# Attention's output projection as three single passes with high and low parts

## The reference

```python
h = h + 0.5 * swiglu(rms_norm(h, g_ffn1), w1_gate, w1_up, w1_down)
h = h + hybrid_mixer(rms_norm(h, g_mix), ...)      # ends in: return o @ w_out
h = h + 0.5 * swiglu(rms_norm(h, g_ffn2), w2_gate, w2_up, w2_down)
...
# second block, much later, needs
ada = silu(c) @ ada_w + ada_b                      # 1024 x 6144 weights
```

## Time and profile before

| what | us |
|---|---|
| median of three runs | 1572.23 |
| lowest, highest | 1571.33, 1572.71 |
| the profiled execution | 1573.47 |
| span of its trace | 1571.5 |
| PE busy in it | 1459.9 (93%) |
| DVE busy | 1049.8 (67%) |
| ACT busy | 546.4 (35%) |
| POOL busy | 563.6 (36%) |

### The profile page before, as it was taken

The page is one execution under the profiler, slowest core; times in us unless marked ns, Lnnn a source line. Parts: engine busy times, 40 slices in busy tenths (PEclk is TensorE's granted clock), DMA queues, the critical chain, the costliest instruction groups (busy, mean ns, idle before and its releaser), DMA issues.

```text
span 1571.5 us, 22748 instructions
## 1 busy us (share of the span) xinstructions
PE 1459.9 (93%) x8272; PEld 1120.8 (71%) x8272; DVE 1049.8 (67%) x2170; ACT 546.4 (35%) x1128; POOL 563.6 (36%) x382
## 2 busy tenths in 40 slices
PE   8999999999999999999999999998988988888777
PEld 7999998767999999998989985444444443333333
DVE  6655376875734328998976468785858585858556
ACT  5444353363544436443134242221212121212114
POOL 2455428220344441001002234554545444444451
PEclk9999999999999999999999999999999998999999
DMA  9888958996999997999976969999999999999996
GB/s 365 312 329 317 348 217 338 315 326 241 407 372 371 376 376 294 374 398 342 362 281 226 401 244 403 404 427 427 427 427 426 427 427 427 427 427 427 426 428 267
DMA packets 99814, 571.91 MB, mean 364 GB/s; under 512 B 11536, under 2 KB 11664, under 8 KB 50448
## 3 DMA queue, kind: packets, MB, share of 16 engines
q1 hardware_dynamic: 61056, 298.15, 51.3%
q0 software_dynamic: 37520, 268.47, 40.7%
q10 hardware_dynamic: 1152, 4.16, 0.7%
HBM read 569.67 MB, written 135.27 MB: 449 GB/s over the span
## 4 chain that ended last, share of the span: by engine, by line
PE 57%; DMA 26%; DVE 6%; SPq 5%; POOL 3%; issue 2%; ACT 1%; ACTq 0%; POOLq 0%; DVEq 0%
DMA arena<-pairs,eidx 15%; PE ps L2727 10%; PE ps L2113 8%; PE ps L2112 8%; PE ps L2111 8%; DMA ring<-pairs,eidx 6%; PE ps L2504 5%; SPq L664 3%; PE ps L2200 2%; PE ps L2198 2%; PE ps L2199 2%; DMA arena<-in_ada 2%; POOL w_lo L754 2%; SPq L663 2%; PE ps L2619 2%
## 5 line engine op out<-in xcount | busy, mean ns | idle before, releaser
L2727 PE MATMUL ps<-arena 128*128 128x512 f32 x844 | 402.6, 626 | 69.1 <-ACT arena L1252 69.1
L2727 PEld LDWEIGHTS ps<-arena 128*128 128x128 f32 x844 | 165.8, 201 | 289.0 <-issue 192.8
L1965 DVE CUSTOM_DVE_ANT_0 arena<-arena 128x1024 f32<-128x1024 f32 x211 | 255.2, 1225 | 145.3 <-DMA arena<-pairs,eidx 144.1
L822 POOL DMA_INDIRECT arena<-pairs,eidx x210 | 244.3, 1163 | 257.1 <-PE ps L2727 208.4
L754 POOL TENSOR_TENSOR w_lo<-ring,w_hi 128x1024 fp32r<-128x1024 f32 x76 | 207.9, 2738 | 257.7 <-DVE w_lo L1305 171.3
L2111 PE MATMUL ps<-u_hi,w_hi 128*128 128x256 f32 (+1 forms) x912 | 259.4, 284 | 1.8 <-POOL w_lo L754 1.5
L2113 PE MATMUL ps<-u_hi,w_lo 128*128 128x256 f32 (+1 forms) x912 | 259.6, 285 | 0.0
L2112 PE MATMUL ps<-u_lo,w_hi 128*128 128x256 f32 (+1 forms) x912 | 259.2, 284 | 0.0
L842 ACT ACTIVATE w_hi<-ring 128x1024 fp32r<-128x1024 f32 x188 | 197.8, 1056 | 149.7 <-PE ps L2200 71.2
L2111 PEld LDWEIGHTS ps<-u_hi,w_hi 128*128 128x128 f32 x912 | 172.1, 189 | 3.2 <-issue 2.3
L2113 PEld LDWEIGHTS ps<-u_hi,w_lo 128*128 128x128 f32 x912 | 172.3, 189 | 0.0
(11 more groups left out here) (394 smaller groups left out, 2505.3 us busy)
## 6 DMA issues: line engine op xcount, KB each, us to landing
ring<-in_stream SPq DMA_DIRECT2D x121, 1024.0 KB, 7.0
pairs<-in_peer_u SPq DMA_DIRECT2D x128, 512.0 KB, 7.5
pairs<-in_peer_v SPq DMA_DIRECT2D x128, 512.0 KB, 8.6
arena<-in_ada SPq DMA_DIRECT2D x32, 768.0 KB, 6.4
arena<-in_stream SPq DMA_DIRECT2D x8, 1024.0 KB, 9.9
arena<-pairs,eidx POOLq DMA_INDIRECT x210, 19.7
h<-in_x_t SPq DMA_DIRECT2D x2, 544.0 KB, 4.7
ring<-in_stream SPq DMA_DIRECT2D x2, 512.0 KB, 7.1
```

The source lines that it names most:

```text
L822: pool.indirect_dma_start(slot_of(n), None, pairs, own).then_inc(landing(n)[0], 16)
L1965: dve.tensor_tensor_reduce(row, row, hf[:, n % HEAD_ROWS // TOPK, :], 1.0, 0.0, ALU.mult, ALU.add, dots[:, n % HEAD_ROWS:n % HEAD_ROWS + 1 ...
L2727: mm = pe.matmul(ps[:, Y_BANKS[j // TOPK] + half, :], diag[:, n % DIAGS, :], slot_of(n)[:, D + half * 512:D + half * 512 + 512], start=(hd ...
```

## The change

1. w_out runs through `split_tile`, from `att_hi` and `att_lo`: `heads_out` (ACT) now writes the high part straight from PSUM, and the new `heads_low` (DVE) subtracts it from PSUM for the low part, one per pair of units. `weigh(m)` waits for the low part of pair m - 2 instead of the copy.
2. The first piece of w_out (`EARLY`, 41) is split during attention, into buffers of its own: ACT copies its halves after the exponentials of units 8 and 12, POOL subtracts (after its 16 small DMAs have landed).
3. The other three pieces and ffn2's first one are split behind attention: `out_high` on ACT (four halves ahead of the first tile of h, the others between tiles), first halves `low` on DVE between the adds, second halves `low` on POOL.
4. The last eight `ada_add` stand one to a tile instead of two, the first of them ahead of the last two `heads_low`; the loads of the first two stand ahead of the 27 `pair_up`.

```diff
+        EARLY = BASE["w_out"]
+        EARLY_AT = (8, 12)
...
             at = FIRST_BLOCKS
+            for q in range(2):
+                load_ada(KT // 2 + 2, q)
             for n in range(BEFORE_ADA):
                 pair_up(at + n)
             at += BEFORE_ADA
-            with sp.Fori(0, KT // 2 - 2) as kt:
-                for q in range(ADA_Q):
-                    load_ada(kt + (KT // 2 + 2), q)
...
+            for n in range(2, 2 * ADA_Q):
+                load_ada(KT // 2 + 2 + n // ADA_Q, n % ADA_Q)
...
+            pool.wait_ge(cum_in, 2 * HEADS * 16)
+            for e in range(2):
+                pool.wait_ge(hi_done, half_number(0, EARLY, e + 1))
+                pool.tensor_tensor(early_lo[:, e, :], ring[:, EARLY % RING, e * HALF:(e + 1) * HALF], early_hi_f[:, e, :], ALU.subtract
+                                   ).then_inc(used if e else lo_done, 1)
+            each_piece(pool, EARLY + 1, BASE["ffn2"] + FFN_P + 1 - EARLY, lambda piece, slot, turn: low(1, piece, slot, 1))
...
+            def out_high(half):
+
+                piece = EARLY + 1 + half // 2
+                high(0, piece, piece % RING, piece // RING, half % 2)
...
+                    for half in range(4):
+                        out_high(half)
...
-                    if n == 2 and k == 4:
...
+                    if n == 2 and k in (1, 2, 4, 5):
+                        out_high((1, 2, 4, 5).index(k) + 4)
...
-                act.activation(oT[:, hd // 2, t * P:(t + 1) * P], ps[:, 5 + m % 2, 0:P], ACT.Copy).then_inc(o_ev, 1)
+                act.activation(att_hi[:, hd // 2, t * P:(t + 1) * P], ps[:, 5 + m % 2, 0:P], ACT.Copy).then_inc(o_hi_done, 1)
...
+                if n in EARLY_AT:
+                    e = EARLY_AT.index(n)
+                    act.wait_ge(landed[EARLY % RING], EARLY // RING * 16 + 16)
+                    act.activation(early_hi[:, e, :], ring[:, EARLY % RING, e * HALF:(e + 1) * HALF], ACT.Copy).then_inc(hi_done, 1)
...
+            def heads_low(m):
+
+                hd, t = head_tile(2 * m)
+                own = slice(t * P, (t + 1) * P)
+                dve.wait_ge(o_hi_done, m + 1)
+                dve.tensor_tensor(att_lo[:, hd // 2, own], ps[:, 5 + m % 2, 0:P], att_hi_f[:, hd // 2, own], ALU.subtract
+                                  ).then_inc(o_lo_done, 1)
...
+                if n >= 6 and n % 2 == 0:
+                    heads_low((n - 6) // 2)
                 scale_p(n)
+            heads_low(units // 2 - 3)
+            ada_add(KT - 2, 0)
+            for m in range(units // 2 - 2, units // 2):
+                heads_low(m)
+            dve.wait_ge(lo_done, EARLY + 1)
+            low(0, EARLY + 1, (EARLY + 1) % RING)
+            lows = {1: EARLY + 2, 3: EARLY + 3, 5: BASE["ffn2"]}
             for m in range(KT):
-                for i in range(2 * m, 2 * m + 2):
-                    if i < 2 * ADA_Q:
-                        ada_add(KT - 2 + i // ADA_Q, i % ADA_Q)
...
+                if m + 1 < 2 * ADA_Q:
+                    ada_add(KT - 2 + (m + 1) // ADA_Q, (m + 1) % ADA_Q)
+                dve.wait_ge(half_used, half_number(0, EARLY + m // 2, m % 2 + 1))
...
                 if m:
                     raw_low(2, m - 1, V("g_ffn2", m - 1))
-                if m == 5:
-                    low(1, BASE["ffn2"], BASE["ffn2"] % RING)
+                if m in lows:
+                    low(0, lows[m], lows[m] % RING)
...
-                pe.wait_ge(landed[slot], piece // RING * 16 + 16)
-                for e in range(2):
-                    m = 2 * p + e
-                    for b in range(KT):
-                        mm = pe.matmul(ps[:, m, 0:SEQ], blk(slot, e * KT + b), oT[:, b, 0:SEQ], start=(b == 0), stop=(b == KT - 1))
-                    mm.then_inc(used if e else wo_mm, 1)
+            for m in range(KT):
+                piece = EARLY + m // 2
+                split_tile(ps[:, m, 0:SEQ], 0, piece, piece % RING, m % 2, SEQ,
+                           (lambda b: pe.wait_ge(o_lo_done, TT * (b + 1))) if m == 0 else None, (att_hi, att_lo),
+                           (early_hi, early_lo) if piece == EARLY else None)
```

More of the change, by code:

```diff
@@ L315, in program @@
         probsT = sq[:, 2:8, 0:2 * P].rearrange("p (a b) (c t) -> p a c b t", a=2, c=2)
-        oT = praw[:, 0:KT, 0:SEQ]
+        place(phase + KT * T)
+        att_hi, att_hi_f = parts("att_hi", KT, SEQ)
+        assert spot[0] <= split
+        place(parts_end)
+        early_hi, early_hi_f = parts("early_hi", 2, HALF)
+        early_lo, _ = parts("early_lo", 2, HALF)
+        assert spot[0] <= act_end - RING * T
+        att_lo = nc.alloc_sbuf_tensor_at("att_lo", [P, KT, SEQ], F32R, offset=u_at)[:, :, :]
+        EARLY = BASE["w_out"]
+        EARLY_AT = (8, 12)
+        UNITS = 2 * HEADS * TT
+        ATT_TILES = UNITS // 2
         place(0)
@@ L568, in program @@
         GAPS = [0]
-        GAPS.append(BASE["ffn2"] - BASE["w_out"])
-        GAPS.append(GAPS[1] + BASE["w_b"] - BASE["z_gate"])
+        GAPS.append(0)
+        GAPS.append(BASE["w_b"] - BASE["z_gate"])
         def half_number(part, piece, e):
@@ L886, in norm @@
                     act.activation(dst[:, k, 0:w], h[:, k, c], ACT.Square).then_inc(sq_done, 1)
-                    if n == 2 and k == 4:
-                        piece = BASE["ffn2"]
-                        for e in range(2):
-                            high(1, piece, piece % RING, piece // RING, e)
+                    if n == 2 and k in (1, 2, 4, 5):
+                        out_high((1, 2, 4, 5).index(k) + 4)
                 for part in between:
@@ L2443, in _ @@
             weigh(units // 2 - 1)
-            pe.wait_ge(o_ev, units // 2)
-            for p in range(4):
-                piece = BASE["w_out"] + p
-                slot = piece % RING
-                pe.wait_ge(landed[slot], piece // RING * 16 + 16)
-                for e in range(2):
-                    m = 2 * p + e
-                    for b in range(KT):
-                        mm = pe.matmul(ps[:, m, 0:SEQ], blk(slot, e * KT + b), oT[:, b, 0:SEQ], start=(b == 0), stop=(b == KT - 1))
-                    mm.then_inc(used if e else wo_mm, 1)
+            for m in range(KT):
[3 more added lines that the diff above has]
+                           (early_hi, early_lo) if piece == EARLY else None)
             ffn(1)
```

33 lines of the change are left out of this document (9 added, 24 removed).

## The result

The changed kernel takes 1581.3 us (median of 4 runs, 1580.2 to 1583.0) against 1571.8 (4 runs, 1570.1 to 1572.7). The ratio on record is 1.0070, 95% interval 1.0057 to 1.0082; it is not the quotient of the two medians, which is 1.0061, and by it the difference is 11.0 us (9.0 to 12.9). The kernel is slower, as forecast, but by 9.5 to 11 us in place of 5.4. The profiled execution took 1581.27 us, span 1579.5, against 1573.47 and 1571.5.

The account below looks back on a forecast made before the run. PE was taken to bound attention, PE's w_out and DVE's chain of adds together the stretch behind. Attention's 0.8 + 3.1 + 1.0 = 4.9 us plus 0.5 gave +5.4, 1577.6 us; range 1570.5 to 1581.5.

Parts of the forecast that it names:

- the stretch behind attention: From the last scaling to the end of ffn2's first tile: 41.5 us instead of 41.0, so +0.5 us.
- (d): In attention: the granted clock falls after a stall, costing 1 us, between 0 and 2.
- The product: w_out on PE: three passes a block, 22.5 us instead of 29.55, 7 us less work.
- (a): In attention: `heads_low` on DVE, one per pair of units, costs 0, at most 1 us.
- (b): In attention: two copies on ACT beyond its slack cost 0.8 us in all, at most 2.
- (c): In attention: POOL's two subtractions hold up DVE's scalings, 3.1 us in all, between 0 and 4.8.
- rival 3: More clock falls, in attention and ffn2's first tile, and a late piece: +9.2 us, 1581.4 us; chance 0.08.
- The shift passes on to the end: From ffn2's first tile on: PE is busy throughout, so a shift of that tile reaches the end unchanged.
- Rivals 1 and 2: Attention doesn't stall, 1573.5 or 1570.5 us, chance 0.23; PE's gain arrives behind attention, 1566.5 us, chance 0.08.

Follow-up runs that it names:

- e3: The changed kernel with each of POOL's two early subtractions cut into eight of 128 columns: 1575.3 us.
- e4: The kernel before with ACT's two early copies and POOL's two early subtractions added, their results unused: 1574.5 us.
- f1: The changed kernel with ffn2's first load issued ahead of the last six loads of ada: 1577.7 us.
- a2: The changed kernel again, unaltered, for a second profile: 1579.3 us.
- b3: The kernel before again, unaltered, for a second profile: 1569.4 us (one execution).
- h1: The kernel before with four products of a constant on PE, three in unit 1 and one ahead of the last weighing: 1569.5 us.
- b4: The kernel before again, unaltered, for a third profile: 1568.9 us (one execution).
- e2: The changed kernel with six products of a constant on PE, three each ahead of the transposes of units 12 and 13: 1576.7 us.
- g1: The changed kernel with early subtractions sliced, ffn2's first load ahead of ada's last six, second halves' low parts of pieces 42 to 44 on DVE: 1569.3 us.
- g2: g1 with four products of a constant on PE, three in unit 1 and one ahead of the last weighing: 1567.7 us.
- f4: The changed kernel with e2's products of a constant and f1's early load: 1575.1 us.

## Why the prediction was right in sign and short in size

Two terms of the sum were too small. The step that failed is the subtraction that gave the stretch behind the attention "+0.5 us": it took 41.0 us as what the kernel before needs there, while that one execution held 3.8 us of a clock fall and a late load, and the term measures 4.0 us. The other is the clock, (d), taken as 1 us and between 0 and 6.25 us in the profiles. The medians give 1581.3 us, just under the upper end of the range, 1581.5; the recorded ratio on 1572.23 gives 1583.2, above it.

- **The product** gives PE 7 us: right as a length of work, and lost in waits as forecast, but not in the same ones. Forecast were waits of 1, 3 and 1.4 us ahead of tiles 4, 6 and 7 of w_out and 3.7 ahead of ffn2; measured are 0.85, 0.77 and 0.86 ahead of tiles 5, 6 and 7, and 3.88.
- **(a) and (b), `heads_low` and ACT's copies:** 0.8 forecast, at most 0.65 measured (e3). Right.
- **(c), POOL's subtractions:** 3.1 forecast. Measured 3.0 for (a), (b) and (c) together, so at least 2.4 for (c); e4, which has (b) and (c) alone, has 2.6. Mechanism and size right: the scalings were held until POOL's end, and PE was at a wait both times. POOL began at 341.6, not 339.2, and ran both in one go.
- **(d), the clock:** mis-sized. The sum took 1 us "over about 3 us" of low clock; in the profiled execution it cost 6.25, over 14 us (in f1 3.0, over 7 us; in a2 none). The pace was off too: work that takes 14 less 6.25 us at full clock took 14, a factor of 1.8 and not 1.4. The duration was taken from one fall in the profile of before, where PE ran three products of a constant, 256 columns wide, for 2.54 us of the low stretch (326.89 to 329.43), and not only the small products of the units. Nothing in the rows said that it would recover as soon among small ones. The estimate should have had a wide upper end, up to the whole of the attention that was left.
- **The stretch behind the attention:** 41.5 us forecast from the end of the last scaling to the end of ffn2's first tile, 41.2 measured (the next tile starts at 414.63, the scaling ended at 373.47). Its working by DVE's order was nearly right: the tile started at 33.3, not 34.5, since the load was issued at 24.5, not 26; the clock fall behind PE's wait, which only rival 3 had, took that back. The step that failed is the other side of the subtraction, "instead of 41.0: +0.5 us". The 41.0 came from one execution; b3, h1 and e4, with before's order there, have 3.8 us less, b4 2.35 less. Against 40.33 in place of 44.16 the term is +4.0 (44.36 less 40.33), not +0.5. The prediction had both signs of it in its own rows, a 29.55 us w_out and a wait of 4.77 us for a load of ada, and took both as the kernel's own.
- **The sum.** What every profile of the changed kernel has, and none of before needs to have: 3.0 us in units 8 to 16 and 4.2 behind the attention (44.5 less 40.33), 7.2 in all. The medians differ by 9.5 us, and by 8.0 in the runs beside a2 (11.0 and 8.6 by the ratios); e2, whose profile has the 7.2 us and no fall behind the stalls, is 5.9 us above the kernel before, 6.8 by its ratio. The 1 to 4 us that the changed kernel has beyond 7.2 should be the falls behind the stalls, less those that the kernel before has of its own; that share is worked out, not measured. With 4.2 in place of 0.5 the sum would have been 9.1.
- **The shift passes on to the end:** right. Ada's sums come 8.57 us later, the end 8.0. What follows ada's sums takes 1161.0 to 1162.6 us in the three profiles of before and 1162.0 and 1162.5 in the two of after.
- **Rival 3** named 1581.4, the time that came. Of its parts the clock was one, though it fell for longer rather than twice, and behind the wait ahead of ffn2 it fell too (0.81 and 0.77 from 404 to 412). The piece did not land late: ACT could start on it 6.3 us after its issue, against 6.2 forecast. So its time was near for causes that are only in part its own, which is luck.
- **Rivals 1 and 2** are out: the attention stalls, and PE's gain doesn't arrive until POOL, SP and DVE are rearranged (g1, g2).

## What to carry to other kernels

Cut a GpSimd instruction that runs beside a VectorE chain on the critical path into short ones, or give it to VectorE; its length, not its sum, is what the chain pays. Before you subtract a stretch of one profiled execution, look whether that execution had a clock fall or a late load in it, and price the stretch without them; equal stretches in two profiles are no proof that the change is free there. A load that others are ordered behind, and that waits for a busy engine's steps, delays all the rest: put the load whose buffer is free ahead of it.

## What was not expected of the hardware

- The granted clock stayed at its lower level for 14 us in work that the profile lists as fully busy (348 to 362: 4.00 us of 4, 20 to 25 products each). In f1 it came back after 7 us, in units 0 to 8 of the profiles that have a fall there after 3 to 7.
- Behind two waits of PE of 0.54 to 1.18 us the clock fell in some executions and not in others: it cost 6.25, 3.0, 0, 0 and 0 us in five profiles. With products of a constant in the stalls it stayed up behind them in both profiles that have them (e2, and f4, where only half of them stood in a wait).
- Such events are part of a kernel's own run-to-run spread of 3 to 10 us, but not all of it: over the seventeen profiles of the table unit 0 starts between 325.66 and 327.88, and what follows ada's sums takes 1160.7 to 1164.9 us. In three profiles of the kernel before, the stage of units 0 to 8 took 10.64, 10.88 and 9.20 us, the one behind the attention 44.16, 40.33 and 41.81, and the two between them 9.63 and 18.81 to within 0.01.
- Sixteen subtractions of 128 columns took POOL 8.45 us with their waits for each other, 0.46 us each in the median; two of 1024 columns took 4.66 us, 2.34 each.
